# A fused decoder block whose first stage multiplies with an unshifted h, its shift added later as a bias

## What is computed

```python
c_act = jax.nn.silu(c)
mod = c_act @ w_ada[l] + b_ada[l]
sh1, sc1, gt1, sh2, sc2, gt2 = jnp.split(mod, 6, axis=-1)
h = _modulate(_rmsnorm(x, norm1_g[l]), sh1, sc1)   # h * (1 + scale) + shift
p = h @ w_in[l]
conf_in, sc_in, gate_in = jnp.split(p, [2 * D_CONF, 2 * D_CONF + 3 * D_SC], axis=-1)
u = conf_in + b_glu[l]
u_a, u_b = jnp.split(u, 2, axis=-1)
u = u_a * jax.nn.sigmoid(u_b)
u = _causal_dwconv(u, conf_dw_w[l]) + conf_dw_b[l]  # width 31
u = jax.nn.silu(_layernorm(u, conf_ln_g[l], conf_ln_b[l]))
y_a = u @ conf_w_out[l] + conf_b_out[l]
g_b, g_c, v = jnp.split(sc_in, 3, axis=-1)
v = g_b * _causal_dwconv(g_c * v, sc_dw_w[l])       # width 3
y_b = v @ sc_w_out[l]
```

## Time and profile before

| | us |
|---|---|
| median of three runs | 919.83 (919.8 to 920.33) |
| profiled execution, whole time | 919.7 |
| its span, slowest core (core 7) | 918.1 |
| spans of all cores | 916.6 to 918.1 |
| PE busy | 872.6 (95%) |
| DVE busy / ACT busy | 464.0 (51%) / 313.0 (34%) |

### The profile page before, as it was taken

How to read it: one execution, slowest core, us unless ns; L and a number is a source line. 1 busy time by engine, 2 the same in 40 slices (tenths; PEclk the granted TensorE clock), 3 DMA queues, 4 the chain that set the end, 5 groups by cost and what they waited for, 6 DMA issues and landing times.

```text
span 918.1 us, 13082 instructions; the slowest of 8 cores (916.6 to 918.1 us)
## 1 busy us (share of the span) xinstructions
PE 872.6 (95%) x4463; PEld 400.6 (44%) x4463; DVE 464.0 (51%) x715; ACT 313.0 (34%) x478; POOL 39.0 (4%) x64
## 2 busy tenths in 40 slices
PE   3599999999999999999999999999999999999996
PEld 0134344444444444444444444444444444444455
DVE  2756646676665656657742212372123532124678
ACT  3565866655422222237751111101110011112333
POOL 0012210000000000000110000000000000000000
PEclk9699999999999999999999999999999999999998
DMA  8986489331658735285008112131122211101225
GB/s 253 282 212 171 98 141 190 79 86 21 186 117 259 198 106 148 69 188 134 1 1 138 35 34 46 34 59 36 35 46 46 47 34 35 30 6 35 85 100 184
DMA packets 29154, 91.92 MB, mean 100 GB/s; under 512 B 3233, under 2 KB 13729, under 8 KB 24866
## 3 DMA queue, kind: packets, MB, share of 16 engines
q1 hardware_dynamic: 23618, 59.26, 21.5%
q0 software_dynamic: 5184, 31.57, 20.4%
q10 hardware_dynamic: 288, 0.26, 0.1%
HBM read 105.73 MB, written 8.39 MB: 124 GB/s over the span
## 4 chain that ended last, share of the span: by engine, by line
PE 85%; DMA 5%; DVE 3%; SPq 2%; issue 2%; ACT 2%; POOL 0%; DVEq 0%; ACTq 0%; POOLq 0%
PE ps L354 66%; PE ps L1015 16%; DMA arena<-wada 3%; PE ps L701 3%; SPq L423 2%; ACT arena L333 2%; DMA arena<-w 2%; DVE arena L336 1%; DVE arena L340 1%; DMA arena<-xc 1%; PE ps L550 1%; POOL arena L464 0%; PE ps L447 0%; ACT L333 0%; SPq L369 0%
## 5 line engine op out<-in xcount | busy, mean ns | idle before, releaser
L354 PE MATMUL ps<-arena 128*128 128x512 bf16 (+1 forms) x3028 | 661.2, 380 | 8.9 <-DMA arena<-cb 2.6
L354 PEld LDWEIGHTS ps<-arena 128*128 128x128 bf16 (+1 forms) x3028 | 296.3, 98 | 368.6 <-issue 14.6
L336 DVE TENSOR_TENSOR arena<-ps,arena 128x512 bf16<-128x512 f32 (+1 forms) x156 | 107.7, 691 | 305.1 <-PE ps L354 221.7
L333 ACT ACTIVATE arena<-arena 128x512 bf16<-128x512 f32 (+3 forms) x217 | 135.6, 651 | 147.7 <-DVE arena L340 78.9
L340 DVE SCALAR_TENSOR_TENSOR arena<-ps,arena 128x512 f32<-128x512 f32 (+2 forms) x184 | 133.4, 727 | 83.5 <-PE ps L1015 41.4
L333 ACT ACTIVATE arena<-ps 128x512 f32<-128x512 f32 x110 | 65.3, 595 | 301.0 <-PE ps L354 300.9
L1015 PE MATMUL ps<-arena 128*128 128x512 bf16 (+1 forms) x800 | 154.0, 353 | 0.0
L336 DVE TENSOR_TENSOR arena<-arena 128x512 f32<-128x512 f32 (+4 forms) x199 | 122.8, 641 | 32.5 <-ACT arena L333 19.2
L333 ACT ACTIVATE arena<-ps,arena 128x512 f32<-128x512 f32 (+1 forms) x125 | 81.9, 688 | 128.8 <-PE ps L354 114.4
L1015 PEld LDWEIGHTS ps<-arena 128*128 128x128 bf16 x800 | 78.2, 98 | 74.3
L340 DVE SCALAR_TENSOR_TENSOR arena<-arena 128x512 f32<-128x512 f32 (+2 forms) x75 | 51.9, 699 | 21.2 <-ACT arena L333 16.6
(11 more groups left out here) (18 smaller groups left out, 35.9 us busy)
## 6 DMA issues: line engine op xcount, KB each, us to landing
arena<-wada SPq DMA_DIRECT2D x48, 512.0 KB, 8.2
arena<-w POOLq DMA_DIRECT2D x21, 1024.0 KB, 10.8
arena<-arena SPq DMA_DIRECT2D x64, 130.0 KB, 2.9
arena<-xc SPq DMA_DIRECT2D x8, 1024.0 KB, 9.5
arena<-xc SPq DMA_DIRECT2D x4, 2048.0 KB, 17.7
arena<-wd POOLq DMA_DIRECT2D x8, 768.0 KB, 7.6
outT<-arena SPq DMA_DIRECT2D x24, 256.0 KB, 2.4
arena<-w POOLq DMA_DIRECT2D x6, 512.0 KB, 9.3
```

The lines of the kernel that those rows point to most:

```text
L333: sch.op("act", lambda e: e.activation(out=out, in_=in_, func=func, **kw), reads=reads, writes=writes)
L336: sch.op(eng, lambda e: e.tensor_tensor(out=out, in0=in0, in1=in1, op=op), reads=reads, writes=writes)
L354: fns.append(lambda e, lt=lt, rh=rh, i=i: e.matmul(bank[b], lhsT=lt, rhs=rh, start=(i == 0), stop=(i == n - 1)))
```

## The change

The scale pieces of w_ada (8 of them) are loaded first, behind x for r=0 and 1; each shift piece follows into the same buffer once its scale was reduced. `stream` and the units for slot B work on h without shift (`in_hs`). Their 16 results are copied to SBUF without bias (`raw_out`, every fourth on DVE). When all shifts exist, shift @ w_in is computed for both slots by 16 matmuls of 32 columns (`shift_rows`), turned into columns by four small f32 matmuls (`shift_cols`), added to b_glu, and used as the bias in `glu_raw`. h of r=0 and 1 is then made again with the shift (`in_h`, 16 operations). w_in's third unit for `sc_unit` gets a slot of its own (F), which lies over x of r=1; x of r=2 waits for slot E and x of r=3 for slot F. `sc_unit(1, 0)` and `(1, 1)` move ahead of `load_xsh(0)`, so that three instead of four `sc_unit` stand between `conv_a(1)`, `(2)` and `(3)`.

```diff
+        def crit_scale(k):
+            STT(wada[k], wada[k], 1.0, cact, ALU.mult, ALU.mult, [B_wada[k], B_cact], [B_wada[k], B_sc[k]], accum_out=mod[:, 8 + k:9 + k])
+            STT(gm[:, k:k + 1], mod[:, 8 + k:9 + k], vecs[:, C_G1 + k:C_G1 + k + 1], bp1[:, k:k + 1], ALU.mult, ALU.add,
+                [B_sc[k], B_bp1, B_vec], [B_gmc[k]])
...
+            load_x(1, 0)
             load_x(1, 1)
-            for k in range(2, KD):
-                tok = crit_load(k)
-                if k == 6:
-                    tok_c6 = tok
-            sch.wait_tok("pool", tok_x1)
+            tok_sc = [crit_load(8 + k) for k in range(KD)]
+            tok_sh = [None] * KD
+            sch.wait_tok("pool", (s_x[0][0], 16))
             load_half(0, 0)
             load_half(0, 1)
...
+            crit_shift(5)
+            u_raw(2, 1)
+            in_h(0, 4, "act")
+            in_h(0, 5, "act")
+            crit_shift(6)
+            in_h(0, 6, "act")
+            u_raw(3, 1)
+            crit_shift(7)
...
+            shift_rows()
+            in_h(0, 7, "act")
+            for k in range(KD):
+                in_h(1, k, ("act", "dve", "act", "act", "dve", "act", "dve", "act")[k])
+            load_slot("F", w8_d[3])
             sch.wait_tok("sp", tok_e)
+            load_x(2, 0)
+            load_x(2, 1)
...
+            sc_unit(0, 0, (shift_cols, None))
+            glu_raw(0, 0)
+            sc_unit(0, 1)
+            in_sq(2, dve=(3, 7))
+            glu_raw(1, 0)
...
+            sc_unit(1, 0, (None, hook2))
+            glu_raw(2, 0)
+            glu_raw(3, 0)
+            sc_unit(1, 1)
...
             conv_a(1)
             conv_b(1)
-            for r in range(NR):
-                sc_unit(1, r)
+            sc_unit(1, 2)
+            sc_unit(1, 3)
+            sc_unit(2, 0)
             flush()
             conv_a(2)
+            conv_b(2)
             load_slot("SWO", w4_d[1])
-            conv_b(2)
-            for r in range(NR):
+            for r in range(1, NR):
                 sc_unit(2, r)
             flush()
```

More of the change, by code:

```diff
@@ L455, in in_tmp, with in_hs @@
             TT(xk, xk, rs1[r % 2], ALU.mult, [B_xst[r][k], B_rs1[r % 2]], [B_xst[r][k]])
+        def in_hs(r, k):
+            out = hbuf[:, k * S + r * TU: k * S + (r + 1) * TU]
+            ACT(out, xst[r][:, k * TU:(k + 1) * TU], AF.Copy, [B_xst[r][k], B_gmc[k]], [B_h[k][r]], scale=gm[:, k:k + 1])
         def in_h(r, k, eng):
@@ L652, in stages @@
                 stream(k, 0)
                 for kk in lag.get(k, ()):
-                    in_h(1, kk, "dve" if kk == KD - 1 else "act")
+                    in_hs(1, kk)
                     stream(kk, 1)
[L656 to L661, removed]
@@ L662, in stages, with raw_out, u_raw @@
-            tok_x2 = load_x(2, 0)
-            load_x(2, 1)
-            sch.wait_tok("pool", tok_x2)
+            gl = {"i": 0}
+            def raw_out(j, r, q, b):
+                n = r * 8 + j * 2 + q
+                if n % 4 == 1:
+                    sch.op("dve", lambda e: e.tensor_copy(out=raw[n], in_=bank[b]), reads=[B_bank[b]], writes=[B_raw[n]])
+                else:
+                    ACT(raw[n], bank[b], AF.Copy, [B_bank[b]], [B_raw[n]])
+            def u_raw(j, r):
+                for q in range(2):
+                    b = next_bank()
+                    MM(b, *w8h_unit(1, (j % 2) * 2 + q, r))
+                    raw_out(j, r, q, b)
@@ new lines, in glu_raw, with shift_rows @@
+            def glu_raw(j, r):
+                i = gl["i"] % 2
+                gl["i"] += 1
+                n = r * 8 + j * 2
+                ACT(sig[i], raw[n], AF.Sigmoid, [B_raw[n], B_bgl], [B_sig[i]], bias=bgl[:, 4 + j:5 + j])
+                STT(upad[:, j * UW + 32 + r * TU: j * UW + 32 + (r + 1) * TU], raw[n + 1], bgl[:, j:j + 1], sig[i], ALU.add, ALU.mult,
+                    [B_raw[n + 1], B_sig[i], B_bgl], [B_u[j][r]])
+            def shift_rows():
+                w0 = slot_ap["A"].rearrange("p (k c) -> p k c", c=512)
+                w1 = slot_ap["B"].rearrange("p (q k c) -> p k q c", q=2, c=256)
+                fns = []
+                for kk in range(4):
+                    for g in range(4):
+                        k = (g % 2) * 4 + kk
+                        rhs = w0[:, k] if g < 2 else w1[:, k]
+                        fns.append(lambda e, g=g, k=k, kk=kk, rhs=rhs: e.matmul(
+                            bank[6][32 * g:32 * g + 32, :], lhsT=shb[:, k * 32:(k + 1) * 32], rhs=rhs, start=(kk == 0), stop=(kk == 3)))
+                sch.pe_group(fns, reads=[B_shb] + B_slh[0] + B_slh[1], writes=[B_bank[6]])
+                sch.op("dve", lambda e: e.tensor_copy(out=srow, in_=bank[6]), reads=[B_bank[6]], writes=[B_srow])
@@ new lines, in shift_cols @@
+            def shift_cols():
+                sch.pe_group([lambda e, n=n: e.matmul(bank[7][:, 2 * n:2 * n + 2], lhsT=srow[:, n * 128:(n + 1) * 128], rhs=sel,
+                                                      start=True, stop=True) for n in range(4)],
+                             reads=[B_srow, B_sel], writes=[B_bank[7]])
+                cols = bank[7][:, 0:8].rearrange("p (j q u) -> p q u j", q=2, u=2)
+                for q, c0 in ((1, 0), (0, 4)):
+                    o3, v3 = [a[:, c:c + 4].rearrange("p (u j) -> p u j", u=2) for a, c in ((bgl, c0), (vecs, C_BGLU + c0))]
+                    TT(o3, cols[:, q], v3, ALU.add, [B_bank[7], B_vec], [B_bgl])
@@ L665, in stages @@
+            crit_shift(0)
+            crit_shift(1)
+            for r in range(2):
+                for blk in range(4):
+                    raw_out(blk // 2, r, blk % 2, r * 4 + blk)
+            sch.wait_tok("pool", tok_sh[3])
             tok_e = load_half(2, 0)
             load_half(2, 1)
+            crit_shift(2)
+            crit_shift(3)
+            u_raw(2, 0)
+            crit_shift(4)
+            u_raw(3, 0)
+            for k in range(4):
+                in_h(0, k, "act")
+            crit_shift(5)
@@ L828, in sc_unit @@
                     rd + [B_vec, B_acc[i]], [B_acc[i]])
+                if hooks[1] is not None:
+                    hooks[1]()
                 b = next_bank()
@@ L836, in in_apply @@
                     in_tmp(r, k)
[L837 to L843, removed]
+                    in_h(r, k, "pool" if k in (1, 4) else "act")
+            sc_unit(0, 0, (shift_cols, None))
[3 more added lines that the diff above has]
+            glu_raw(1, 0)
             def hook2():
@@ L858, in stages @@
             u_unit(3, 2)
-            tok_xsh = conv_a(0)
+            for j in range(1, 4):
+                glu_raw(j, 1)
+            conv_a(0)
             conv_b(0)
@@ L889, in stages @@
             bg_init()
[L890 removed]
+            load_slot("A", w8_d[6])
             def reload_x(r):
```

137 lines of the change are left out of this document (67 added, 70 removed).

## The result

| | before | after |
|---|---|---|
| median | 919.82 us | 940.41 us |
| runs | 919.38 to 920.33 | 938.87 to 941.77 |
| ratio, 95% interval | 1 | 1.0223 (1.0202 to 1.0244) |
| profiled execution, whole time | 919.7 | 938.87 |
| its span, slowest core | 918.1 | 937.3 |

A forecast was written before the change was run, and what follows sets the result against it. PE's work was taken as nearly fixed, so the result was the sum of its holes: 919.7 - 1.7 + 5.8 = 923.8, put at 923.9 us since the median lies 0.1 higher. Own range 921.7 to 926; 8 in 10, 916.5 to 928.

The forecast's parts named there:

- Stream's end: End of PE's streamed matmuls in the opening: at 52.2 us, 4.5 us earlier than before.
- Slot B and the shift: After the stream: slot B's units end at 66.1, shift matmuls at 66.7, `sc_unit(0, 1)` at 79.7; lead 3.6 us.
- Slot F: Load over x of r=1: lands at 82.1, PE there at 81.4, 0.7 us lost; x of r=2 could add 2.
- Norm of r=2: Before `u_unit(0, 2)`: h ready at 94.9 or 95.2, PE waits 2.5 us, using 1.4 more of the lead.
- First convolution: Copies start at 98.1, land by 110.9; PE loses 0.5 us, ends at 118.0, then loses 2.4 and 0.8.
- The opening: Everything up to the second wide convolution's end: 153.4 instead of 155.1 us, 1.7 us gained.
- Three units: Three `sc_unit` instead of four between convolutions: PE waits 3.05 and 2.75 us at two returns, 5.8 lost, bounds 0 and 7.4.
- The step that failed: Slots, gates and everything behind: only renamed, costing nothing while POOL loads a slot well ahead.
- (1): Lag taken up: opening gives its 1.7 us, waits at `st_a` under 1 us each; 918.1, down to 914; chance 0.27.
- (2): Half the loss at the returns: one return waits, or each 1.5 us; 920.3 us; chance 0.18.
- (3): Opening gains nothing: half clock 2 us, slot F behind x 2, shift columns 2.5; 927 to 930 us; chance 0.1.

The follow-up runs named there:

- the kernel with both waits: Changed kernel with POOL again waiting for the shifted copies before loading slot A and before loading SWO and CWO: 927.16 us, ratio 1.0057.
- the kernel with SWO's wait alone: Changed kernel with only the loads of SWO and CWO held until the copies of r=2 have landed: 931.99 us, ratio 1.0110.

## Why the prediction was wrong, point by point

- **Stream's end** 52.2, lead 4.5: measured 52.8, lead 3.9. Right.
- **Slot B and the shift**: units' end 66.1, measured 66.75; the shift's 16 matmuls at 66.7 for 0.9 us, measured 67.55 for 1.05; the small f32 matmuls 1.5 us, measured 0.95 (the trace has eight of them for four). `sc_unit(0, 1)` ends at 71.18 + 40 x 0.216 = 79.8 for 79.7. Right, by two small errors of opposite sign.
- **Slot F**: 0.7 lost, measured 0.37 (and 1.54 for DVE in its place in the kernel with both waits). Right.
- **Norm of r=2**: PE on again at 94.9 or 95.2 with 2.5 us lost; measured 95.56 and 2.98. Right in place. Unpriced: in six of the eight profiled cores that have this wait (those of after and of the experiments that leave it) a stretch at the lower clock follows, 11.9 to 13.4 us instead of 10.5 for 48 matmuls (below).
- **First convolution** starting at 110.9, ending at 118.0: measured 113.08 and 120.2, since the copies started at 99.6 for 98.1 and took 13.3 for 12.7. It costs nothing more: ACT was forecast to free the next bank at 120.3 and does so at 120.2, so the 2.4 + 0.8 us put as lost there are 0.16. PE reaches the second convolution at 145.8 in after and 147.2 in the kernel with both waits, forecast 146.3; that convolution ends at 154.3 there, forecast 153.4, before 155.1. **The opening gains 0.8 us there, forecast 1.7.** These are the slowest cores, core 7 in both traces; on core 0 the gain is 0.9, on core 5 1.4, and on core 2 there is none.
- **Three units**: with both waits back, the evictions start 178.96 - 154.26 = 24.7 us behind the convolution's end (24.8 forecast), the return waits 2.57 us (3.05) and the next one 1.66 (2.75), 4.2 for 5.8. In the changed kernel itself the first is swallowed by the wait for the copies, the second stands at 2.60. Right mechanism, slightly too large.
- **The step that failed** is the sentence "Slots, gates and everything behind are only renamed, and cost nothing while POOL loads a slot well ahead". I asked whether the slots arrive in time for their readers, and they do. I did not ask what else is on the transfer engines when they leave. The change took out the wait of POOL for the copies and bound SWO to slot E; this costs 15.3 us by the ratios (14.7 by the medians) of the 16.5 by which the result lies over the forecast. The same question had been asked at two other places, for x beside slot A and for slot F beside x, the latter with 2 us as the bound; and the Trainium skill ("DMA: Bandwidth & Descriptors", Issuing engines are not separate DMA queues), cited there for its harmless side, says that transfers of all issuers interleave on the same 16 engines. The trace agrees, 14.5 and 16.8 us for a copy that takes 2.6 on its own.
- **Rivals**: none had this. (1), the lag taken up, and (2), half of it, are refuted by the kernel with both waits: its returns wait 2.57 and 1.66 us, 4.2 in all, where (1) allowed under 1 us each and (2) one wait or 1.5 each; (3) named a transfer behind a transfer at slot F alone, and of its three parts the lower clock came, at another place.
- **The forecast without the failed step**, 0.44% above before, against 0.57% (0.42 to 0.72) for the kernel with both waits: inside its interval. On that kernel's core 7 the terms are 0.8 gained (1.7 forecast, and 1.6 of lower clock already in it), 4.2 lost at the returns (5.8) and 1.7 of lower clock behind the first of them (not forecast): 5.1 us, against 0.57% of 920, 5.2, which is also how far apart PE's last matmuls stand in the two traces (910.26 and 915.47). The total fits better than its terms: what the lower clock took, the smaller returns gave back, and that is luck.

## What to carry to other kernels

A wait of an issuing queue for something that it doesn't read may be there to keep big loads off small transfers that an engine is waiting for: before removing one, or before binding a load to another buffer, write down when each load will leave now and which latency-bound copies are in flight then, and price the overlap from a stretch of the same trace where it already happens. When a stretch of cover is shortened, follow the lag to its end: moved units take the wait along, here past two returns to the gates.

## What the runs showed of the hardware

**A wait of some 3 us can be followed by half clock.** Stretches of the kernel with both waits (core 7): length, PE busy with its count, granted clock, share of the transfer engines, GB/s.

```profile
93.50:96.50 3.00, 0.17 (x1) 0.97 0.00 0
96.50:98.50 2.00, 1.95 (x5) 0.50 0.00 0
98.50:100.50 2.00, 2.00 (x8) 0.69 0.03 8
...
181.40:184.00 2.60, 0.06 (x1) 1.00 0.87 164
184.00:186.00 2.00, 1.97 (x8) 0.77 1.11 219
186.00:188.00 2.00, 2.00 (x6) 0.50 1.12 224
```

PE had worked without a hole from 83.15 to 93.7 and stood for 2.88 us; then the clock is 0.50, its lower level of 1.2 GHz, and back at full in the stretch from 100.5 on. That costs 1.6 us on top of the wait (12.09 for 10.52). Behind the 2.57 us at 181.4 it costs 1.7 (14.80 for 13.11). It isn't so every time: the changed kernel's core 5 waits 2.98 us at the same place and goes on at full clock (10.52), and so do three cores of the kernel with SWO's wait alone behind 2.57 to 2.62 us (13.11). What decides it, these runs don't show. Such a wait should be priced with 0 to 2.9 us more than its length, the ends seen here; behind the wait of 10.15 us it was 2.6.

**Small copies suffer far more than loads do.** Beside the copies, the four slots of after landed in 11.4 to 16.7 us. Held back behind them in the kernel with both waits, the same four took 8.8 to 15.9, and one alone 10.2. The copies beside them went from 2.6 to 14.5 us and more.
